# The last four modulations of an encoder trunk, and three smaller orders of its queues

## The chip, the core and the metric

The kernel runs on one core of a Trainium2 chip. Its time is the device time of the program in microseconds (us), the median of the runs. One execution of it was taken by the hardware profiler; all rows below are of that one. Engines are named as the profile names them: PE is TensorE's matmuls and PEld its weight loads, DVE is VectorE, ACT ScalarE, POOL GpSimd, SP the SyncE queue that issues every load and store.

## The reference, cut to what matters

One inference step of a trunk of two layers over 2048 prompt tokens and 32 sample tokens, D_MODEL 1024, float32. Layer 0 is a pooling mixer (windows of 2, 4, 8 and 16 tokens for four groups of 256 channels), layer 1 sliding-window attention with 16 heads and 4 key/value heads. Each branch has a gate path beside it, and each layer is modulated by a vector of the conditioning input c:

```python
def modulation(c, w, b):
    m = jnp.einsum('bd,de->be', jax.nn.silu(c), w) + b
    return jnp.split(m, 3, axis=-1)
...
        for i in range(DEPTH):
            shift, scale, gate = modulation(c, ada_w[i], ada_b[i])
            h = rms_norm(x, norm_g[i]) * (1 + scale[:, None]) + shift[:, None]
            ...
            x = x + gate[:, None] * y
        return rms_norm(x, final_g), ...
```

So a layer needs three modulations of 1024 values for the prompt's c and the same for the sample's: two vectors of 1024 times a matrix of 1024 x 1024, six times in all.

## The kernel before

**Stages.** The prompt is cut into four parts of 512 tokens; part 0 also carries the 32 sample tokens and so has two blocks of 272 columns where the others have one of 512. Activations lie transposed, channels on partitions. The stages are pooling parts 0 to 3, then attention parts 0 to 3. A projection unit is one output tile of 128 channels against all eight input tiles k. Every product of two float32 values is made of three fp32r products (high times high, high times low, low times high; `split_product`, L921), so a unit of 512 columns is 24 matmuls, and it has one PSUM bank of three, `ps_u`, in turn.

**A pooling part** goes through four groups g. A group has the units u0 and u1 (projection tiles `pin`), gate0 and gate1, and two short units z0 and z1 (6 matmuls each) that mix the pooled channels; then come eight output units and the turning of the next part's x. As banks go round by three and z0, z1 follow gate0 and gate1, the next group's u0 takes the bank of gate1. On VectorE a unit's first evacuation (step E1) scales the bank by the norm (L1308); a gate's second (E2) multiplies its silu product into `silu_g` (L1337), and with that the bank is free; PL pools (L1352 to L1377) and PQ subtracts the high part of the pooled tile from it (L1384). Around gate0 VectorE's order is E1 of gate0, PQ, PL, E2 of gate0, PQ, E1 of gate1. After a z unit VectorE multiplies and subtracts again (L1332).

**An attention part** has twenty projection tiles and eight output tiles (`aout`), of which the first four (five in part 0) are kept open in parallel while the last heads finish.

**The hand-made order.** Class `Schedule` writes one list of steps, and every engine walks that list and does its own share of each step, with waits on semaphores that count steps. So where a step stands in the list sets its place in every engine's queue, SP's among them.

**Weights.** A tile is 128x1024. It goes into slot j % RING of four. Tile j is asked for (step WL) right after the last unit that uses tile j - 4. The first time it is loaded raw, split by ScalarE (a copy to the high part, L1525) and GpSimd (the subtraction, L1785) and stored to HBM as two tiles; later it is fetched from there. 24 of the attention tiles are split early, eight in each of pooling parts 1 to 3: step FL loads one raw (L744), FW splits it on ScalarE (L1529) and GpSimd (L1792), FS stores it. There are two buffers for this, so the load of tile i + 2 waits, on SP, for the store of tile i; FL stands right behind the FS before it in the list:

```python
            i = EARLY // 3 * (p - 1) + n
            self.steps.append(("FS", i))
            if i + FORE < EARLY:
                self.steps.append(("FL", i + FORE))
```

**Modulations.** Their weights come in 48 chunks of 512 KB, eight for each modulation. The first 16 chunks are used at the start. The other 32 are spread over the pooling parts, eight steps ADA in each: behind u0 and u1 of groups 0 and 1, behind u1 of group 2 and behind gate0 of groups 0, 1 and 2. A step is four matmuls of 128x32 against 256 columns of the chunk (L952) that sum into a bank of `ps_s`. After a modulation's eight steps ScalarE copies the sums out (step MR, L1538), and in group 3, behind gate0, step MT turns the row of sums into a column with eight matmuls (L964). Three chunk buffers, `load_ada` (L792) issues the next load on SP at each ADA step.

**Waits of a unit.** Before a unit TensorE waits for its tile's weights, and ahead of each k for both halves of that input tile, although these are complete after the first unit of a stage.

## Time and profile before

| what | value |
|---|---|
| median of 3 runs | 1661.25 us (1660.24 to 1665.72) |
| the profiled execution's own time | 1663.97 us |
| its span in the profile | 1662.2 us |
| mean granted TensorE clock | 0.983 |
| HBM | 266.13 MB read, 74.31 MB written, 205 GB/s over the span |

In the page's chain of waits, the chain of work that ended last, TensorE holds 75% of the span, DMA 7%, VectorE 6%, ScalarE 4%. Rows below have these columns: in an order-of-time answer the start in us, the duration in us, engine, line, operation, written tile <- read tiles, shapes, the number of instructions, and in brackets the idle time before it with what ended it. In a table of stretches a number in front of "(x...)" is the busy time in us and the number in brackets is the count of instructions; the last three are the granted clock, the share of DMA engines' time that is busy and the GB/s moved. A product of 128 x 512 is shown with a modelled end; from start to start is the better reading.

### The profile page before, as it was taken

How to read it: one execution, taken by the hardware profiler on the slowest of the kernel's cores; microseconds unless marked ns; L12 is line 12 of the kernel's file. 1: busy time of each engine (PE TensorE's matmuls, PEld its weight loads, DVE VectorE, ACT ScalarE, POOL GpSimd, SP SyncE). 2: the span in 40 equal slices, each digit the busy share in tenths (PEclk: the TensorE clock that was granted, in tenths of full speed). 3: DMA queues.
4: the chain of work that ended last, by engine and by line, in shares of the span. 5: the costliest groups of instructions: out<-in, count | busy, mean ns of one | idle time of the engine just before them, and what ended most of it. 6: DMA issues, size and time to landing. Idle time of an engine off the chain costs nothing.

```text
span 1662.2 us, 28381 instructions
## 1 busy us (share of the span) xinstructions
PE 1572.7 (95%) x9355; PEld 1319.7 (79%) x9355; DVE 826.7 (50%) x2154; ACT 729.9 (44%) x1618; POOL 421.6 (25%) x403
## 2 busy tenths in 40 slices
PE   5899999989999999999889899999899998999997
PEld 2899987777777877888888798888788887888876
DVE  2556335323434344336666634666346664366651
ACT  3444433223232333235555454656436664456642
POOL 0342421112111211112222241333213333123332
PEclk9899999999999999999999999999999999999998
DMA  8787788886888778962222275334463334643313
GB/s 286 267 291 262 265 302 289 299 318 229 281 325 286 272 278 289 335 242 103 103 104 102 102 256 188 142 129 153 151 203 128 128 137 167 211 149 129 131 67 135
DMA packets 174519, 342.10 MB, mean 206 GB/s; under 512 B 22127, under 2 KB 89023, under 8 KB 174126
## 3 DMA queue, kind: packets, MB, share of 16 engines
q1 hardware_dynamic: 174382, 340.29, 58.4%
q8 instruction: 84, 1.38, 0.3%
q14 instruction: 53, 0.43, 0.1%
HBM read 266.13 MB, written 74.31 MB: 205 GB/s over the span
## 4 chain that ended last, share of the span: by engine, by line
PE 75%; DMA 7%; DVE 6%; ACT 4%; issue 3%; SPq 2%; POOL 1%; POOLq 0%; DVEq 0%; ACTq 0%
PE ps_u L921 59%; DMA w_lo_kept<-fore_raw 4%; PE ps_o L1153 4%; PE ps_s L1107 3%; PE ps_t L1126 3%; ACT work L1726 1%; DMA work<-in_x_prompt_dram 1%; DVE work L1453 1%; PE ps_s L921 1%; ACT ps_u L1625 1%; PE ps_s L952 1%; DMA chunks<-in_ada_w_dram 1%; DMA w_raw<-in_pool_w_out_dram 1%; PE ps_t L1166 1%; DVE ps_u L1308 1%
## 5 line engine op out<-in xcount | busy, mean ns | idle before, releaser
L921 PE MATMUL ps_u<-h_all_hi,w_hi 128*128 128x512 f32 (+2 forms) x1440 | 520.4, 361 | 11.9 <-DVE h_all_lo L1238 4.4
L921 PE MATMUL ps_u<-h_all_lo,w_hi 128*128 128x512 f32 (+2 forms) x1440 | 511.2, 355 | 0.0
L921 PE MATMUL ps_u<-h_all_hi,w_lo 128*128 128x512 f32 (+2 forms) x1440 | 510.8, 355 | 0.0
L921 PEld LDWEIGHTS ps_u<-h_all_hi,w_hi 128*128 128x128 f32 x1440 | 274.2, 190 | 66.5 <-issue 22.7
L921 PEld LDWEIGHTS ps_u<-h_all_hi,w_lo 128*128 128x128 f32 x1440 | 274.1, 190 | 36.9
L921 PEld LDWEIGHTS ps_u<-h_all_lo,w_hi 128*128 128x128 f32 x1440 | 274.1, 190 | 34.5
L1308 DVE TENSOR_TENSOR ps_u<-ps_u,rstd_b 128x512 f32<-128x512 f32 (+1 forms) x180 | 107.1, 596 | 274.4 <-PE ps_u L921 266.9
L921 PE MATMUL ps_u<-y_hi,w_hi 128*128 128x512 f32 (+1 forms) x600 | 218.4, 364 | 16.0 <-issue 10.6
L1866 POOL TENSOR_TENSOR work<-work,recip 128x512 f32<-128x512 f32 (+2 forms) x136 | 132.9, 997 | 360.3 <-DVE recip L1470 360.3
L921 PE MATMUL ps_u<-y_hi,w_lo 128*128 128x512 f32 (+1 forms) x600 | 213.2, 355 | 0.0
L921 PE MATMUL ps_u<-y_lo,w_hi 128*128 128x512 f32 (+1 forms) x600 | 212.6, 354 | 0.0
L1726 ACT ACTIVATE work<-work,neg_max 128x256 f32<-128x256 f32 (+1 forms) x272 | 132.1, 487 | 109.1 <-DVE sink_arg L1461 109.1
L1625 ACT ACTIVATE ps_u<-ps_u,wb 128x272 f32<-128x272 f32 (+1 forms) x144 | 73.2, 521 | 160.1 <-DVE ps_u L1308 159.5
L921 PEld LDWEIGHTS ps_u<-y_hi,w_hi 128*128 128x128 f32 x600 | 114.2, 190 | 36.8 <-issue 20.3
L921 PEld LDWEIGHTS ps_u<-y_lo,w_hi 128*128 128x128 f32 x600 | 114.3, 190 | 16.4 <-issue 1.4
L921 PEld LDWEIGHTS ps_u<-y_hi,w_lo 128*128 128x128 f32 x600 | 113.7, 189 | 16.1
L1792 POOL TENSOR_TENSOR fore_raw<-fore_raw,fore_hi 128x1024 fp32r<-128x1024 f32 x24 | 57.5, 2397 | 252.0 <-ACT fore_hi L1529 252.0
L1785 POOL TENSOR_TENSOR w_lo<-w_raw,w_hi 128x1024 fp32r<-128x1024 f32 (+1 forms) x32 | 72.3, 2262 | 145.6 <-ACT w_hi L1525 145.6
L1453 DVE CUSTOM_DVE_ANT_0 work<-ps_s,bias 128x256 f32<-128x256 f32 (+1 forms) x272 | 95.7, 407 | 1.4
L1817 POOL TENSOR_TENSOR acc<-acc,sq 128x512 f32<-128x512 f32 (+1 forms) x48 | 62.7, 1307 | 130.3 <-ACT sq L1667 130.3
L1845 POOL TENSOR_TENSOR y_lo<-acc,y_hi 128x256 fp32r<-128x256 f32 (+1 forms) x72 | 49.2, 684 | 182.2 <-ACT y_hi L1752 182.2
L1625 ACT ACTIVATE work<-ps_u,wb 128x512 f32<-128x512 f32 (+3 forms) x48 | 25.4, 549 | 136.4 <-DVE ps_u L1308 136.4
(210 smaller groups left out, 2237.1 us busy)
## 6 DMA issues: line engine op xcount, KB each, us to landing
w_hi<-w_hi_kept SPq DMA_DIRECT2D x180, 512.0 KB, 4.1
w_lo<-w_lo_kept SPq DMA_DIRECT2D x180, 512.0 KB, 5.2
chunks<-in_ada_w_dram SPq DMA_DIRECT2D x32, 512.0 KB, 6.1
w_hi_kept<-w_hi SPq DMA_DIRECT2D x28, 512.0 KB, 3.3
w_lo_kept<-w_lo SPq DMA_DIRECT2D x28, 512.0 KB, 4.4
w_hi_kept<-fore_hi SPq DMA_DIRECT2D x24, 512.0 KB, 9.1
w_lo_kept<-fore_raw SPq DMA_DIRECT2D x24, 512.0 KB, 10.0
w_raw<-in_pool_w_in_dram SPq DMA_DIRECT2D x16, 512.0 KB, 5.9
```

Source lines behind the costliest of these rows:

```text
L921: last = nc.tensor.matmul(out, w, x, start=(i == 0), stop=(i == n - 1))
L1107: last = nc.tensor.matmul(score_block(it, at + e, k0), q_st[half, q, c0:c0 + P], k[half, d, kc], start=(i == 0), stop=(i == 2))
L1126: last = nc.tensor.transpose(t_flat[:, o:o + P], work[:, a % 2, at * 256 + kt * P:at * 256 + (kt + 1) * P], ident[:, :])
L1153: last = nc.tensor.matmul(ps_o[:, n * 256:n * 256 + 256], v_st[:, d, t + kt, :], pt[:, o:o + 256], start=(i == 0), stop=(i == 2 * len(kts) ...
L1308: V.tensor_tensor(bank[:, 0:w], bank[:, 0:w], rstd_b[:, c0:c0 + w], ALU.mult).then_inc(scaled, 1)
L1453: last = V.tensor_tensor_reduce(out=out, in0=src, in1=b, scale=HEAD_DIM ** -0.5, scalar=LOWEST, op0=ALU.add, op1=ALU.max, accum_out=row_ma ...
L1625: last = A(dst, src, ACT.Identity, bias=wb[:, u["n"], v:v + 1])
L1726: A(x, x, ACT.Exp, bias=neg_max[r, d, at:at + 1], accum_out=row_sum[r, d, at:at + 1])
L1785: G.tensor_tensor(w_lo[:, j % RING, 0:width[j]], w_raw[:, j % RING, 0:width[j]], w_hi[:, j % RING, 0:width[j]].bitcast(F32), ALU.subtract) ...
L1792: G.tensor_tensor(raw.bitcast(F32R), raw, fore_hi[:, i % FORE, :].bitcast(F32), ALU.subtract).then_inc(fore_lo_ready, 1)
L1817: G.tensor_tensor(acc[:, 0:w], acc[:, 0:w], sq[:, 0:w], ALU.add).then_inc(acc_ready, 1)
L1866: last = G.tensor_tensor(x, x, recip[r, d, 2 * n:2 * n + 2].unsqueeze(2).to_broadcast([r.stop - r.start, 2, w]), ALU.mult)
```

## The change

- **Modulations.** Chunks from the 17th on are read as 128 whole rows of `ada_w` (128x1024, contiguous). VectorE takes the ADA step in TensorE's place: for each of the two vectors one operation of 128x1024 multiplies the chunk by a per-partition scalar and adds it to a sum (`mod_sum`) that lies in the x buffer which is free in that part. It signals `ada_added`. Step MT then sums over partitions and turns at once, with sixteen matmuls of 128x128 against a column of ones. Step MR goes for these modulations. New waits: the buffer's earlier content must be stored and squared before the first sum of a modulation, and the next x, and the load of x for attention, wait for `mod_turned`.
- **Early tiles.** FL is no longer behind FS. It stands behind gate0 of the group (for the FS behind u1) or behind the z units (for the FS behind gate1).
- **Tile requests.** The fourth `aout` tile of each attention part goes to a fifth slot that lies in the query buffer `q_st`; it is asked for behind the part's last scores step (S). The other tiles keep the ring of four, counted without it.
- **Unit waits.** TensorE waits for a tile's weights ahead of the tile's first block only, and for the input halves of each k only in the first unit and the first output unit of a stage.

The core of the diff; what is left out passes `slot_of[j]` where `j % RING` stood, waits for `ada_added` where all modulations must be done, and renames a local variable:

```diff
-        load_after = {self.last_unit[j - RING]: j for j in range(RING, len(self.tiles))}
+        self.slot, self.before, held, at = [], [], {}, 0
+        for j, t in enumerate(self.tiles):
+            n = RING
+            if t != ("aout", 3):
+                n, at = at, (at + 1) % RING
+            self.slot.append(n)
+            self.before.append(held.get(n))
+            held[n] = j
+        load_after = {("U", self.last_unit[self.before[j]]): j for j in range(len(self.tiles)) if self.slot[j] < RING and self.before[j] is not None}
+        for j, t in enumerate(self.tiles):
+            if t == ("aout", 3):
+                p = self.units[self.last_unit[j]]["p"]
+                load_after[("S", max(x["a"] for x in self.items if x["p"] == p))] = j
         steps, self.steps = self.steps, []
         for st in steps:
             self.steps.append(st)
-            if st[0] == "U" and st[3] == KT and st[1] in load_after:
-                self.steps.append(("WL", load_after[st[1]]))
+            if (st[0] == "S" or st[0] == "U" and st[3] == KT) and st[:2] in load_after:
+                self.steps.append(("WL", load_after[st[:2]]))
...
             self.steps.append(("ADA", i))
-            if i % KT == KT - 1:
+            if i % KT == KT - 1 and i < self.first:
                 self.steps.append(("MR", i // KT))
 
     def early(self, p, n):
@@ -181,10 +193,13 @@
     def early_out(self, p, n):
 
         if p:
-            i = EARLY // 3 * (p - 1) + n
-            self.steps.append(("FS", i))
-            if i + FORE < EARLY:
-                self.steps.append(("FL", i + FORE))
+            self.steps.append(("FS", EARLY // 3 * (p - 1) + n))
+
+    def early_next(self, p, n):
+
+        i = EARLY // 3 * (p - 1) + n + FORE
+        if p and i < EARLY:
+            self.steps.append(("FL", i))
...
                 if i == 0:
+                    self.early_next(p, 2 * g)
                     self.early(p, 2 * g + 1)
                     s.extend(late + [("PQ", p, g, 1)])
...
             s.extend(late + lower + [("E2", late[0][1])])
+            self.early_next(p, 2 * g + 1)
...
+        q_flat = q_st[:, :, :].rearrange("p a c -> p (a c)")
+        tile_hi = [w_hi[:, i, :] for i in range(RING)] + [q_flat[:, 0:KT * P]]
+        tile_lo = [w_lo[:, i, :] for i in range(RING)] + [q_flat[:, KT * P:2 * KT * P]]
...
+        stage_first = set()
+        for stage in range(2 * PARTS):
+            stage_first.add(next(u["u"] for u in units if u["s"] == stage))
+            stage_first.add(next(u["u"] for u in units if u["s"] == stage and u["kind"] == "out"))
...
+        def mod_sum(m, v):
+
+            return x_of(m - 1)[:, 2 * v:2 * v + 2, 0:PART]
...
+                if slot == RING:
+                    p = units[sched.last_unit[j]]["p"]
+                    sp.wait_ge(s_ready, sum(1 for x in items if x["p"] <= p))
+                else:
+                    tile_used(sp, before_in[j])
...
-                    sp.wait_ge(ada_done, i - CHUNKS + 1)
+                    sp.wait_ge(ada_added, i - CHUNKS - first + 1)
+                if i >= first:
+                    k = i % KT
+                    sp.dma_start(landing[slot], I["ada_w"][l, k * P:(k + 1) * P, what * D_MODEL:(what + 1) * D_MODEL]).then_inc(ada_loaded[slot], 16)
+                    return
...
                     if p < 2:
                         sp.wait_ge(mid_stored[p % 2], 2 * 16 * KT)
                         sp.wait_ge(sq_ready, KT * (p + 3))
+                        sp.wait_ge(mod_turned, len(sched.mods))
...
-                elif kind == "ADA":
+                elif kind == "ADA" and st[1] < first:
 
                     i = st[1]
                     m, half, pair = i // KT, i % KT // 4, i % 4
-                    if m >= 2 and i % KT == 0:
...
+                    if m >= 2:
+                        pe.wait_ge(ada_added, KT * (m + 1) - first)
+                        for k in range(KT):
+                            for v in range(2):
+                                last = nc.tensor.matmul(mod_turn[m][:, 2 * k + v:2 * k + v + 1],
+                                                        mod_sum(m, v)[:, k // 4, k % 4 * P:(k % 4 + 1) * P], ones[:, 0:1], start=True, stop=True)
+                        last.then_inc(mod_turned, 1)
+                        continue
...
-                    if own(j):
+                    if u["b"] == 0 and k_from == 0 and own(j):
                         pe.wait_ge(w_hi_ready, splits(j))
                         pe.wait_ge(w_lo_ready, splits(j))
-                    else:
-                        pe.wait_ge(w_fetched[j % RING], 32 * fetches(j))
+                    elif u["b"] == 0 and k_from == 0:
+                        pe.wait_ge(w_fetched[slot_of[j]], 32 * fetches(j))
...
-                            if u["kind"] != "out":
+                            if u["u"] not in stage_first:
+                                pass
+                            elif u["kind"] != "out":
...
+                elif kind == "ADA" and st[1] >= first:
+
+                    i = st[1]
+                    m, k = divmod(i, KT)
+                    p = m - 2
+                    slot, nth = ada_slot(i)
+                    if k == 0 and p == 0:
+                        dve.wait_ge(ada_done, first)
+                        dve.wait_ge(x_squared, TILES + 1)
+                        dve.wait_ge(x_turned, TILES + 1)
+                    elif k == 0:
+                        dve.wait_ge(mid_stored[(p - 1) % 2], 16 * KT * ((p - 1) // 2 + 1))
+                        dve.wait_ge(sq_ready, KT * p)
+                    if k:
+                        dve.wait_ge(ada_added, i - first)
+                    dve.wait_ge(ada_loaded[slot], 16 * nth)
+                    chunk = landing[slot].rearrange("p (a c) -> p a c", a=2)
+                    for v in range(2):
+                        if k == 0:
+                            last = V.tensor_scalar(mod_sum(m, v), chunk, c_wide[:, k, v:v + 1], None, ALU.mult)
+                        else:
+                            last = V.scalar_tensor_tensor(out=mod_sum(m, v), in0=chunk, scalar=c_wide[:, k, v:v + 1], in1=mod_sum(m, v),
+                                                          op0=ALU.mult, op1=ALU.add)
+                    last.then_inc(ada_added, 1)
...
                         dve.wait_ge(x_turned, xt_at[(p, t)] + 1)
+                        if p:
+                            dve.wait_ge(mod_turned, p + 2)
```

## Rows read from the trace of the kernel before

**Rows 1.** Page, busy us of each engine, share of the span, instructions.

```profile
PE 1572.7 (95%) x9355; PEld 1319.7 (79%) x9355; DVE 826.7 (50%) x2154; ACT 729.9 (44%) x1618; POOL 421.6 (25%) x403
```

**Rows 2.** Stretches of pooling parts 1 to 3: length, busy, clock, DMA.

```profile
227.86:400.62 172.76, 165.70 (x761) 128.74 (x760) 64.92 (x114) 50.72 (x78) 29.70 (x17) 0.97 0.81 287
400.62:569.28 168.66, 162.74 (x755) 126.62 (x754) 67.35 (x114) 50.43 (x78) 29.57 (x17) 0.98 0.82 287
569.28:728.86 159.58, 156.66 (x726) 121.96 (x725) 64.45 (x115) 46.18 (x76) 30.22 (x18) 1.00 0.82 291
```

**Rows 3.** The chain that ended last, in order of time: start, length, link.

```profile
161.45 1.68 PE ps_o L964 x16
...
388.79 5.56 PE ps_u L921 x24
...
395.21 11.13 PE ps_u L921 x48
...
408.59 5.77 PE ps_u L921 x24
...
414.93 5.76 PE ps_u L921 x24
```

**Rows 4.** TensorE in order of time, attention output stages 1 to 3.

```profile
1187.02 0.77 PE L921 MATMUL ps_u<-y_hi,w_hi 128*128 128x512 f32 x1 [3.81 <-issue]
...
1405.97 0.47 PE L921 MATMUL ps_u<-y_hi,w_hi 128*128 128x512 f32 x1 [2.87 <-issue]
...
1622.32 0.47 PE L921 MATMUL ps_u<-y_hi,w_hi 128*128 128x512 f32 x1 [2.89 <-issue]
```

**Rows 5.** Waits of SP's queue by line: us in total, times, longest.

```profile
SPq L744 <- DMA w_lo_kept<-fore_raw: 144.2, 15, 10.7
```

**Rows 6.** TensorE in order of time, norm sums; two records are one matmul.

```profile
407.21 0.36 PE L989 MATMUL ps_o<-ones,sq 128*128 128x1 f32 x2
407.43 0.36 PE L988 MATMUL ps_o<-ones,acc 128*128 128x1 f32 x2
```

**Rows 7.** VectorE, groups by line and shape: busy us, mean ns, idle before.

```profile
L1476 DVE TENSOR_TENSOR pt_lo<-ps_t,pt_hi 128x1024 fp32r<-128x1024 f32 x56 | 68.3, 1220 | 1.9 <-ACT pt_hi L1735 1.4
```

**Rows 8.** VectorE in order of time, part 2, group 0.

```profile
424.97 0.69 DVE L1384 TENSOR_TENSOR q_st<-sq,q_st 128x512 fp32r<-128x512 f32 x1 [0.17 <-ACT q_st L1676]
...
427.05 0.70 DVE L1308 TENSOR_TENSOR ps_u<-ps_u,rstd_b 128x512 f32<-128x512 f32 x1 [1.39 <-PE ps_u L921]
```

**Rows 9.** TensorE in order of time, first matmul of part 2, group 1.

```profile
429.85 0.50 PE L921 MATMUL ps_u<-h_all_hi,w_hi 128*128 128x512 f32 x1
```

**Rows 10.** GpSimd in order of time, parts 0 and 2.

```profile
100.66 1.38 POOL L1785 TENSOR_TENSOR w_lo<-w_raw,w_hi 128x512 fp32r<-128x512 f32 x1 [5.74 <-ACT w_hi L1525]
...
107.64 2.40 POOL L1785 TENSOR_TENSOR w_lo<-w_raw,w_hi 128x1024 fp32r<-128x1024 f32 x1 [5.60 <-ACT w_hi L1525]
...
112.16 2.40 POOL L1785 TENSOR_TENSOR w_lo<-w_raw,w_hi 128x1024 fp32r<-128x1024 f32 x1 [2.12 <-ACT w_hi L1525]
...
425.89 2.40 POOL L1792 TENSOR_TENSOR fore_raw<-fore_raw,fore_hi 128x1024 fp32r<-128x1024 f32 x1 [12.91 <-ACT fore_hi L1529]
```

**Rows 11.** VectorE in order of time, part 0, group 1.

```profile
100.83 1.24 DVE L1352 COPY work<-u_keep 128x16 f32<-128x16 f32 x1
...
109.61 0.45 DVE L1308 TENSOR_TENSOR ps_u<-ps_u,rstd_b 128x272 f32<-128x272 f32 x1 [1.46 <-PE ps_u L921]
...
112.52 2.35 DVE L1332 TENSOR_TENSOR y_lo<-acc,y_hi 128x272 fp32r<-128x272 f32 x1
```

**Rows 12.** Stretch behind the first gap of rows 4, columns as above.

```profile
1187.00:1195.50 8.50, 8.48 (x25) 6.73 (x26) 1.43 (x3) 2.58 (x4) 1.70 (x2) 0.66 0.78 318
```

**Rows 13.** TensorE in order of time, inside a unit of part 2.

```profile
409.56 0.40 PE L921 MATMUL ps_u<-h_all_lo,w_hi 128*128 128x512 f32 x1
409.80 0.39 PE L921 MATMUL ps_u<-h_all_hi,w_lo 128*128 128x512 f32 x1
410.03 0.40 PE L921 MATMUL ps_u<-h_all_hi,w_hi 128*128 128x512 f32 x1
```

More of the change, by code:

```diff
@@ L519, in trunk_kernel @@
         t_flat = ps_t[:, :, :].rearrange("p a b -> p (a b)")
-        mod_bank = [ps_u[0][:, :], ps_u[2][:, :]] + [ps_s[:, m % 2, :] for m in range(2, 6)]
+        mod_bank = [ps_u[0][:, :], ps_u[2][:, :]]
         mod_turn = [ps_u[0] if m == 0 else ps_o for m in range(6)]
@@ L534, in trunk_kernel @@
         w_kept = [sem(f"w_kept{i}") for i in range(RING)]
-        w_fetched = [sem(f"w_fetched{i}") for i in range(RING)]
-        w_hi_ready, w_lo_ready, ada_done = sem("w_hi_ready"), sem("w_lo_ready"), sem("ada_done")
+        w_fetched = [sem(f"w_fetched{i}") for i in range(RING + 1)]
+        w_hi_ready, w_lo_ready, ada_done, ada_added = sem("w_hi_ready"), sem("w_lo_ready"), sem("ada_done"), sem("ada_added")
         prm_turned, prm_ready, c_tanh, c_ready, mod_ready = (
@@ L580, in keeps @@
         def keeps(j):
-            return sum(1 for i in kept if i <= j and i % RING == j % RING and own(i))
+            return sum(1 for i in kept if i <= j and slot_of[i] == slot_of[j] and own(i))
         def fore_done(eng):
@@ L587, in fore_done @@
                 eng.wait_ge(fore_kept[i], 32 * sum(1 for n in range(EARLY) if n % FORE == i))
-            eng.wait_ge(ada_done, KT * len(sched.mods))
+            eng.wait_ge(ada_added, KT * len(sched.mods) - first)
         def fetches(j):
-            return sum(1 for i in range(j + 1) if i % RING == j % RING and not own(i))
+            return sum(1 for i in range(j + 1) if slot_of[i] == slot_of[j] and not own(i))
         def tile_used(eng, j):
@@ L753, in load_tile @@
                 t = tiles[j]
-                if j >= RING:
-                    tile_used(sp, j - RING)
-                    if own(j - RING):
-                        sp.wait_ge(w_kept[j % RING], 32 * keeps(j - RING))
-                load_raw(t, w_raw[:, j % RING, :], raw_loaded[j % RING])
+                if before_in[j] is not None:
+                    tile_used(sp, before_in[j])
+                    if own(before_in[j]):
+                        sp.wait_ge(w_kept[slot_of[j]], 32 * keeps(before_in[j]))
+                load_raw(t, w_raw[:, slot_of[j], :], raw_loaded[slot_of[j]])
             def keep_tile(j):
@@ L1060, in _ @@
                             last = split_product(bank[:, 0:w], [
-                                (w_hi[:, slot, k * P:(k + 1) * P], w_lo[:, slot, k * P:(k + 1) * P],
+                                (hi[:, k * P:(k + 1) * P], lo[:, k * P:(k + 1) * P],
                                  xh[:, k, c0:c0 + w], xl[:, k, c0:c0 + w])], k == 0, k == KT - 1)
@@ L1080, in _ @@
                     pe.wait_ge(k_prev, n)
-                    first = 0 if p else 1
-                    for b in range(TILES + 1 - first):
-                        last = nc.tensor.transpose(s_flat[:, b * P:(b + 1) * P], kv_t[:, (first + b) * P:(first + b + 1) * P], ident[:, :])
+                    b0 = 0 if p else 1
+                    for b in range(TILES + 1 - b0):
+                        last = nc.tensor.transpose(s_flat[:, b * P:(b + 1) * P], kv_t[:, (b0 + b) * P:(b0 + b + 1) * P], ident[:, :])
                     if p == 0:
```

43 lines of the change are left out of this document (22 added, 21 removed).

## The prediction

> **What bounds the kernel now.** I read the page's busy shares first: TensorE is busy 95% of the span, VectorE 50% [rows 1]. So a microsecond counts only if it lies on TensorE's line or in one of its gaps. Next the table by stage, cut at the first matmul of each stage, which shows the three pooling parts that carry eight modulation steps each (parts 1 to 3): 172.76, 168.66 and 159.58 us for the same products [rows 2]. Then the chain of waits: a projection unit is 24 matmuls, two in a row take 11.13 us, so 5.57 a unit, and units with a modulation step between them start 6.34 apart [rows 3]. A step costs TensorE 0.77 us. Last, the gaps: in the output stage of the last three attention parts TensorE stands for 3.81, 2.87 and 2.89 us before the fifth output tile [rows 4], and SP spent 144.2 us behind the stores of early-split tiles [rows 5].
>
> The profiled run took 1663.97 us round a span of 1662.2; the median of the runs shown is 1661.25, 2.7 lower. I sum against 1663.97 and take 2.7 off. A measurement of this kernel can tell about 0.3% (5 us) from no change.
>
> **The steps leave TensorE.** 32 steps of 0.77 are 24.6 us, 6.2 in each pooling part (the first part's blocks are narrower, the step the same four matmuls; I take the same price). The four evacuations of row sums on ScalarE go too; nothing waits for them now, so they count nothing.
>
> **The turning gets longer.** Eight turning matmuls, sixteen records, take 1.68 us [rows 3]. Now there are sixteen of 128x128 against one column. The norm's sums are of that very form, and one is issued every 0.22 us [rows 6]: 16 make 3.5. That is 1.8 us more, four times, on TensorE, with nothing beside it: +7.2.
>
> **VectorE gets 64 operations of 128x1024.** The nearest row is the 1024-column split, 1.22 us [rows 7]; one operand there is in PSUM, so this bounds the price from below where a port is contended. A step is 2.4 us, 77 us in all. VectorE's average allows it; what counts is the place. In VectorE's order the third step of a group stands behind the second low-part subtraction (L1384) and ahead of the first evacuation of the second gate unit (L1308). The next group's first projection reuses that gate's bank, so it waits for the gate to be finished. In part 2 the last subtraction starts at 424.97, the second gate's evacuation at 427.05 [rows 8], the next projection at 429.85 [rows 9]: 2.80 us from evacuation to projection. VectorE's slack before it is 1.39 us [rows 8], and without TensorE's step the gate would even end 0.77 earlier.
>
> With 2.4 us of new work from 425.60 (0.63 behind the start of L1384, as operations follow each other in that list) the evacuation would start at 428.0 and the projection at 430.8, 0.95 late. But GpSimd's split of an early tile starts at 425.89 and takes 2.40 [rows 10], between the two halves. What that means is in part 0: GpSimd's split from 112.16 takes 2.40 [rows 10], and a subtraction of two SBUF operands on VectorE, started at 112.52, takes 2.35 for 272 columns [rows 11], ending with it. Both new operands of a step lie in SBUF too. Who goes first when both queue: GpSimd's split at 100.66 [rows 10] stands against a VectorE stream without a gap, and the copy of 16 columns at 100.83 takes 1.24 [rows 11]. So GpSimd gets in between two VectorE instructions. The step is then 1.22, 2.40, 1.22: done at 430.4, projection at 433.2, **3.35 late**. The Trainium skill (SBUF — State Buffer, Who interferes with whom) speaks against this change here: a VectorE instruction with two SBUF inputs contends with a GpSimd one that reads SBUF, and issue order decides who blocks. The rows above agree with it; who goes first when both queue it does not say, and by it alone the sum lies anywhere between my two ends, 1645 and 1680.
>
> So for parts 1 to 3 both ends are +0.95 and +3.35 a group. I take 3.35, since the two rows with both engines waiting look like that. Per part: three groups, 10.05, less five other steps, 3.85, plus 1.8 for turning: +8.0, over three parts **+24.0**. (At the low end: 2.85 - 3.85 + 1.8 = +0.8 each, +2.4.)
>
> Part 0 is tighter, as each unit has two blocks. Between a group's first gate and its last silu product VectorE shows 1.46 us idle that a delay can use up, before 109.61 [rows 11]. Two steps fall into this stretch, 2.4 and, with a split between the halves (at 107.64 one begins where the step would [rows 10]), 4.8: 7.2 - 1.46 = 5.7 us late, in three groups; two more steps saved outside give 1.5 back, turning takes 1.8: **+17.4** (low end, no split between: 3.3 a group, +10.2).
>
> **Clock.** In parts 1 to 3 TensorE then stands 4.2 us nine times (from 429.0 to 433.2). After the 3.81 us gap [rows 4] the granted clock was 0.66 over the next unit, which took 8.4 instead of 5.7 us [rows 12], in part at the 1.2 GHz level; after the gap of 2.87 nothing of the kind is seen. So 0 to 2.7 us each; I take 0.7, **+6**. The longer turning may cost as much once or twice; it stays in the range.
>
> **SP's requests move.** The raw load of the next early tile was issued right behind the store of the one before it in its slot, and held SP, with weight requests and modulation loads queued behind it, until that store had landed [rows 5]. It moves about one unit later (behind the first gate, or the last product pair of a group), past the weight request of that unit and ahead of a modulation load. The store is then nearly done. Parts 1 and 2 are longer than part 3 by 13.2 and 9.1 us [rows 2]; turning the next x explains four times 0.85 of each (units 388.79 and 395.21 apart by 6.42 against 5.57 [rows 3]). The other 9.8 and 5.7 are late tiles, late x and the slow clock behind them. DMA is busy 0.82 there [rows 2], so I give back 14 and 2 more in part 3, whose steps waited on their chunks: **-16** (bounds -8 and -18). The chunk now comes by 4 KB rows and is wanted some 5 us later on VectorE.
>
> **The extra slot.** The fourth output tile goes to the query buffer, asked for once the part's last scores are done; the fifth takes a ring slot free since the last gate. That removes 3.81 + 2.87 + 2.89 = 9.6 [rows 4] and the slow clock behind the first, 2.7 [rows 12], and perhaps some of the third: **-13** (bounds -9.6 and -14). Next there is the bank of the first output tile, evacuated well inside the three short products that follow.
>
> **Unit waits.** TensorE drops up to 16 waits in most units. Within one k, where no wait stands, the third product starts 0.24 us behind the second; the first of the next k, which has the waits, starts 0.23 behind that [rows 13], and 48 in a row take 11.13 [rows 3], 0.232 each over 16 such borders. A wait that is already met shows no price on either side: 0.
>
> New waits on VectorE (stored x, squares, chunk loaded) stand in front of the step, and the evacuations of the next units queue behind them; the store and the chunk are issued a unit or more ahead, so 0, at most the 7 us of one late chunk. x's load for attention waits for all turnings, long done.
>
> Sum: 1663.97 + 24.0 + 17.4 + 6 - 16 - 13 = 1682.4; less 2.7, **1680** for the runs.
>
> **Rivals.** (1) GpSimd does not get in: VectorE's two halves run back to back. For it: they are issued together, and each starts before GpSimd is ready. Against it: the copy at 100.83. Then +2.4 + 10.2 - 16 - 13 = -16.4 and no gap over 2 us, so no clock: 1645, **faster**. It decides at the nine third steps: at 2.4 us the loss per group is 0.95, at 4.8 it is 3.35; nine groups, three of part 0 and the clock grow with it, so the total crosses zero about 16.4 / (12 + 6/2.4) = 1.1 above 2.4, at 3.5 us a step. (2) VectorE's work hides altogether: -24.6 + 7.2 - 29 = -46, 1615. Against it is the 1.39 us of slack for 2.4 of work. (3) SP is held by another wait (the early store, whose split now ends later), and of its 16 us only the 8 of the low bound come back: with the lock 1688. (4) Losses and returns cancel: GpSimd gets in, but only in the six groups of two parts (-7.2), the clock doesn't fall (-6), and part 0 loses half of what lies between its ends (-3.6): 1663.
>
> **Chances.** Forecast 1680 (own range 1667 to 1694, by the bounds) with (3): 0.54. Rival 1: 0.30, a range of 1636 to 1652. Rival 2: 0.06. Rival 4: 0.10, within 5 us of no change. So slower 0.54, same 0.10, faster 0.36. Range 1640 to 1694: it leaves out rival 2, the lowest part of rival 1 and a little above.
>
> **What would show it.** In the new profile the third step of a group should be two operations of 1.2 and 3.6 us with GpSimd's split between, and TensorE should wait 4 us for L1337's product at the end of three groups in each of parts 1 to 3; part 3 should be longer than 159.58, parts 1 and 2 about as long as before. Turning should take 3.5 us, the gap before the fifth output tile should be gone. If those operations are 1.2 and 1.2, rival 1 holds. If part 0 grows by under 10 us, its sum was wrong.

## The result, and the profile after

The changed kernel takes 1699.6 us, the median of 4 runs (1696.0 to 1703.4), against 1663.4 for the kernel before on the same chip: 1.0219 of its time (95% interval 1.0186 to 1.0253), 36 us slower. The forecast was 1680 and 1694 at the upper end of the range; the direction was right and the size was not. The profiled execution took 1703.4 us round a span of 1701.6, which is the longest of the four runs, so its rows show some 4 us more than the median.

The page's busy times of the changed kernel (rows 1 are those of before):

```profile
PE 1585.6 (93%) x9163; PEld 1351.1 (79%) x9163; DVE 923.5 (54%) x2218; ACT 727.2 (43%) x1614; POOL 431.6 (25%) x403
```

VectorE has 97 us more, where 64 operations were added. TensorE has 192 records less (128 matmuls gone and 32 added, two records each) and still 13 us more of busy time. Busy time that grows while work shrinks points at the clock.

The table of stretches of the changed kernel, cut at the first matmul of each stage: pooling part 0, then parts 1 to 3, which answer to [rows 2]. Columns are length, busy time by engine, granted TensorE clock, DMA share and GB/s.

```profile
51.69:256.97 205.28, 183.69 (x1320) 180.59 (x1321) 116.58 (x254) 74.26 (x144) 68.44 (x35) 0.92 0.70 241
256.97:436.00 179.03, 167.30 (x713) 134.96 (x711) 89.15 (x130) 50.08 (x77) 32.76 (x17) 0.92 0.79 277
436.00:610.87 174.87, 163.20 (x708) 132.20 (x707) 91.55 (x130) 49.94 (x77) 32.78 (x17) 0.95 0.80 277
610.87:782.22 171.35, 159.74 (x679) 128.56 (x678) 88.68 (x131) 45.70 (x75) 33.40 (x18) 0.95 0.78 271
```

Part 0 was 178.0 us before (from 49.86 to 227.86) and is 27.3 longer. Parts 1 to 3 are 6.3, 6.2 and 11.8 longer, 24.3 together. The four attention parts are 14.2 shorter (926.7 to 912.5 from the first matmul of the first to TensorE's last). The first projection starts 1.8 later. That is the whole difference of the spans: 27.3 + 24.3 - 14.2 + 1.8 = 39.2 of 39.4. The granted clock of the pooling parts fell from 0.97, 0.98 and 1.00 [rows 2] to 0.92, 0.95 and 0.95.

VectorE in order of time in part 2, group 0, the place that [rows 8] show before (start, duration, instruction, idle time in front):

```profile
458.06 0.68 DVE L1409 SCALAR_TENSOR_TENSOR silu_g<-silu_g,ps_u 128x512 f32<-128x512 f32 x1
458.92 0.69 DVE L1456 TENSOR_TENSOR q_st<-sq,q_st 128x512 fp32r<-128x512 f32 x1 [0.17 <-ACT q_st L1750]
459.53 4.62 DVE L1283 SCALAR_TENSOR_TENSOR x_odd<-chunks,c_wide,x_odd 128x1024 f32<-128x1024 f32 x2
464.07 0.69 DVE L1380 TENSOR_TENSOR ps_u<-ps_u,rstd_b 128x512 f32<-128x512 f32 x1
466.11 0.69 DVE L1409 SCALAR_TENSOR_TENSOR silu_g<-silu_g,ps_u 128x512 f32<-128x512 f32 x1 [1.36 <-ACT silu_g L1715]
```

GpSimd in order of time at the same place, and TensorE's first matmul of the next group:

```profile
459.84 3.22 POOL L1866 TENSOR_TENSOR fore_raw<-fore_raw,fore_hi 128x1024 fp32r<-128x1024 f32 x1 [11.48 <-ACT fore_hi L1601]
```

```profile
466.86 0.79 PE L959 MATMUL ps_u<-h_all_hi,w_hi 128*128 128x512 f32 x1 [3.88 <-DVE silu_g L1409]
```

This is the picture that was forecast. The step's two operations take 4.62 us with GpSimd's split in them (the split itself shows 3.22 instead of 2.40 [rows 10]; it starts behind the step's first operation and waits for it). The second gate is evacuated from 464.07, its silu product follows 2.04 later, and TensorE has stood for 3.88 us. The same stall of 3.8 to 3.9 is there in all nine groups of parts 1 to 3.

What the forecast had nearly left out comes behind the stall. Stretches of 8.6 and 7.3 us that hold the first unit behind two such stalls, in parts 1 and 2, columns as above:

```profile
289.80:298.40 8.60, 8.54 (x25) 6.75 (x26) 2.68 (x5) 1.26 (x2) 0.00 (x0) 0.64 0.71 266
466.80:474.10 7.30, 7.24 (x25) 5.84 (x26) 2.67 (x5) 1.26 (x2) 0.00 (x0) 0.77 0.99 380
```

The unit's 24 matmuls take 7.3 to 8.7 us instead of 5.8, at a mean granted clock between the two levels of 1.2 and 2.4 GHz. Over the nine units it is 17.0 us (2.8, 2.2, 1.6, 1.5, 1.5, 1.5, 2.7, 1.6 and 1.6 longer than the same units before).

Two more things changed as planned. Turning is longer; this is the one of part 3, where 3.67 us for 32 records stood as 3.5 in the forecast. In parts 0 to 2 it is 4.52, 4.14 and 4.89, as the clock falls in the middle of it; the stretch is the second half of the one in part 2, where TensorE is busy throughout at a granted clock of 0.50:

```profile
722.71 3.67 PE L1001 MATMUL ps_o<-ones,x_even 128*128 128x1 f32 x32
```

```profile
549.00:551.30 2.30, 2.30 (x12) 2.30 (x13) 2.10 (x4) 1.03 (x2) 0.00 (x0) 0.50 1.00 371
```

And the gap before the fifth output tile [rows 4] is gone. TensorE in order of time in attention part 1: the last product of the fourth tile, read from the query buffer, and the first of the fifth.

```profile
1235.31 0.40 PE L959 MATMUL ps_s<-y_hi,q_st 128*128 128x512 f32 x1
1235.55 0.40 PE L959 MATMUL ps_u<-y_hi,w_hi 128*128 128x512 f32 x1
```

### The profile page after: what moved, and what is told of

The parts are those of the page before. It is cut to its first block, busy times and chain, and to the rows that moved or that the text cites. A ratio compares the mean times of both kernels' runs of the same rounds, so it can differ in the third digit from the quotient of the medians.

```text
span 1701.6 us, 26049 instructions
## 1 busy us (share of the span) xinstructions
PE 1585.6 (93%) x9163; PEld 1351.1 (79%) x9163; DVE 923.5 (54%) x2218; ACT 727.2 (43%) x1614; POOL 431.6 (25%) x403
## 4 chain that ended last, share of the span: by engine, by line
PE 75%; DVE 12%; ACT 6%; issue 3%; DMA 2%; POOL 1%; SPq 1%; DVEq 0%; ACTq 0%; POOLq 0%
PE ps_u L959 59%; PE ps_o L1199 4%; PE ps_s L1153 3%; PE ps_t L1172 3%; DVE x_odd L1283 2%; DVE x_even L1283 2%; ACT ps_u L1699 1%; PE ps_s L959 1%; ACT work L1800 1%; DVE work L1430 1%; DVE work L1525 1%; DVE ps_u L1380 1%; PE ps_o L1001 1%; PE ps_t L1212 1%; ACT silu_g L1715 1%
## 5 line engine op out<-in xcount | busy, mean ns | idle before, releaser
L959 PE MATMUL ps_u<-h_all_hi,w_hi 128*128 128x512 f32 (+2 forms) x1440 | 531.1, 369 | 48.3 <-DVE silu_g L1409 44.1
L959 PE MATMUL ps_u<-h_all_lo,w_hi 128*128 128x512 f32 (+2 forms) x1440 | 521.9, 362 | 0.0
L959 PE MATMUL ps_u<-h_all_hi,w_lo 128*128 128x512 f32 (+2 forms) x1440 | 521.1, 362 | 0.0
L959 PEld LDWEIGHTS ps_u<-h_all_hi,w_hi 128*128 128x128 f32 x1440 | 282.8, 196 | 91.0 <-DVE silu_g L1409 48.7
L959 PEld LDWEIGHTS ps_u<-h_all_hi,w_lo 128*128 128x128 f32 x1440 | 282.8, 196 | 39.1
L959 PEld LDWEIGHTS ps_u<-h_all_lo,w_hi 128*128 128x128 f32 x1440 | 283.4, 197 | 37.1
L959 PE MATMUL ps_u<-y_hi,w_hi 128*128 128x512 f32 (+1 forms) x584 | 211.9, 363 | 5.5 <-POOL y_lo L1919 5.3
L959 PE MATMUL ps_u<-y_hi,w_lo 128*128 128x512 f32 (+1 forms) x584 | 207.4, 355 | 0.0
L959 PE MATMUL ps_u<-y_lo,w_hi 128*128 128x512 f32 (+1 forms) x584 | 207.1, 355 | 0.0
L1866 POOL TENSOR_TENSOR fore_raw<-fore_raw,fore_hi 128x1024 fp32r<-128x1024 f32 x24 | 66.4, 2766 | 266.7 <-ACT fore_hi L1601 253.1
L959 PEld LDWEIGHTS ps_u<-y_hi,w_lo 128*128 128x128 f32 x584 | 110.4, 189 | 15.7
```

The costliest lines, as they stand in the source:

```text
L959: last = nc.tensor.matmul(out, w, x, start=(i == 0), stop=(i == n - 1))
L1866: G.tensor_tensor(raw.bitcast(F32R), raw, fore_hi[:, i % FORE, :].bitcast(F32), ALU.subtract).then_inc(fore_lo_ready, 1)
```

## The experiments

Two theories stood against each other. **Place**: all that is lost comes from where the VectorE steps stand, as a stall with the slow clock behind it, and the other edits give back time. **Load or other edits**: VectorE has no room for 77 us more wherever they stand, or the moved requests cost something too. Each run below gives its median beside the kernel before on the same chip (1665.6, 1665.1, 1666.7 and 1665.0 in the four sets of runs). The other columns are stage lengths of the profiled execution alone, from first matmul to first matmul, attention up to TensorE's last:

| kernel | median, us | part 0 | parts 1 to 3 | attention |
|---|---|---|---|---|
| before | 1663.4 | 178.0 | 501.0 | 926.7 |
| changed | 1699.6 | 205.3 | 525.3 | 912.5 |
| modulations back on TensorE | 1631.1 | 178.3 | 478.8 | 911.6 |
| before, modulations on VectorE only | 1713.4 | 205.0 | 520.9 | 924.1 |
| changed, third step moved | 1638.9 | 191.7 | 473.5 | 912.2 |
| changed, no split within the third step | 1668.5 | 204.8 | 481.1 | 912.8 |
| changed, two steps moved | 1642.0 | 190.3 | 475.9 | 912.8 |
| before, extra slot only | 1649.9 | 179.0 | 503.4 | 910.7 |
| before, later early loads only | 1643.4 | 178.5 | 478.7 | 925.6 |
| before, unit waits dropped only | 1665.1 | 181.5 | 499.7 | 926.1 |
| changed, early loads back | 1697.4 | 202.6 | 520.8 | 910.9 |
| changed, third step moved, early loads back | 1666.9 | 190.3 | 505.1 | 912.1 |
| changed, matmuls in the stall | 1684.2 | 203.2 | 502.0 | 912.5 |
| TensorE in part 0, VectorE behind z | 1629.1 | 180.7 | 477.1 | 911.9 |
| the same, turning in three | 1623.4 | 181.1 | 471.0 | 911.5 |

### Modulations back on TensorE, the rest kept

```diff
-            if i % KT == KT - 1 and i < self.first:
+            if i % KT == KT - 1:
                 self.steps.append(("MR", i // KT))
...
-                elif kind == "ADA" and st[1] < first:
+                elif kind == "ADA":
...
-                elif kind == "ADA" and st[1] >= first:
...
```

> The changed kernel with its last four modulations on TensorE again as before (steps, evacuation and turning); tile requests, extra slot, later early loads and unit waits stay. Theory 'place' (the VectorE steps cost all that is lost): pooling part 0 is back at 178.0 us, parts 1 to 3 give back 11 against the kernel before (34.4 of stalls + 13.3 of slow clock + 6.2 of turning - 18.2 of steps saved = 35.7 against 24.3 measured), attention gives back 14.2: 1663.4 - 11 - 14 = 1638. Rival 'other edits' (the later requests or the slot cost time too, so the steps cost less than that): above 1655.

Measured: 1631.05 us, 0.9806 of before (0.9786 to 0.9826). Part 0 is back at 178.3. So the other three edits are worth 35 us and the VectorE steps cost 69 on top of them. "Other edits" falls; "place" had the total 7 too high, as parts 1 to 3 give back 22, not 11.

### Only the modulations, on the kernel before

```diff
-                elif kind == "ADA":
+                elif kind == "ADA" and st[1] < first:
...
+                elif kind == "ADA" and st[1] >= first:
```

> The kernel before with nothing but its last four modulations on VectorE. Theory 'place': + 27.3 in part 0 and + 35.7 in parts 1 to 3 = 1726, attention as before. Rival 'other edits': the steps alone cost less, under 1705. If early loads behind the stores hold SP less now that the steps come later, it may lie some 5 below the first figure.

Measured: 1713.4 us, 1.0297 (1.0276 to 1.0319). Part 0 is 27.0 longer, parts 1 to 3 are 19.9 longer, not 35.7. The steps alone cost 48 on the kernel before and 69 on the kernel with the other edits: 48 - 35 would make the changed kernel 1678, and it is 1699.6. Something that the other edits give back is swallowed when the steps are on VectorE.

### The third step of a group behind the second z unit

```diff
-                    if g < 3:
-                        self.ada(1)
-                    else:
+                    if g == 3:
                         s.append(("MT", 2 + p))
...
             self.early_next(p, 2 * g + 1)
+            if g < 3:
+                self.ada(1)
```

> The changed kernel, but the third step of a group stands behind the second z unit instead of behind the first gate; the same 64 operations on VectorE. Theory 'place': TensorE's stall of 3.82 us and the slow unit behind it (1.5 on average) go nine times in parts 1 to 3, 48 us; in part 0 some 5.3 of a group's 8.5 go, three times, and the 3.16 that the second step costs before the second gate's second block stays: 1699.6 - 48 - 16 = 1636. Rival 'load' (VectorE has no room for 77 us more, the delay turns up at the next evacuation): 1690 to 1700.

Measured: 1638.9 us, 0.9848 (0.9833 to 0.9863): the same 64 operations, 12 of the 32 steps moved three units down the list, and 61 us less than the changed kernel. VectorE in order of time behind the z units in part 1 (the last subtraction of the group, the step, the next group's first evacuation):

```profile
275.84 0.69 DVE L1404 TENSOR_TENSOR y_lo<-sq,y_hi 128x512 fp32r<-128x512 f32 x1
276.45 2.48 DVE L1283 SCALAR_TENSOR_TENSOR x_even<-chunks,c_wide,x_even 128x1024 f32<-128x1024 f32 x2
279.74 0.70 DVE L1380 TENSOR_TENSOR ps_u<-ps_u,rstd_b 128x512 f32<-128x512 f32 x1 [0.81 <-PE ps_u L959]
```

Behind the step VectorE waits 0.81 us for TensorE, where TensorE waited 3.88 for it. "Load" falls for parts 1 to 3. In part 0 13.7 us stay.

### GpSimd's split kept out of the third step

```diff
                     pool.wait_ge(fore_hi_ready, i + 1)
+                    if i % 8 in (1, 3, 5):
+                        pool.wait_ge(ada_added, 8 * (i // 8 + 1) + (3, 6, 8)[i % 8 // 2])
```

> The changed kernel, but in parts 1 to 3 GpSimd's second split of a group waits for the third step, so that it doesn't fall between that step's two operations. Theory 'place with the port': the step takes 2.45 us instead of 4.6, TensorE stands 1.7 to 1.8 instead of 3.8 nine times, -19, and the slow units behind the stalls go with it in part or whole, -6 to -13: 1668 to 1675; part 0 as in the changed kernel. Rival 'place alone' (GpSimd's split does not lengthen the step, the two operations take 4.6 anyway): 1699, stalls of 3.8.

Measured: 1668.5 us, 1.0003 (0.9981 to 1.0024), 31 less than the changed kernel. Ten runs lie between 1658.2 and 1670.4 and the profiled one is the shortest, so its table of stages flatters it by 10. VectorE, TensorE and the stretch behind, in part 2, group 0:

```profile
439.79 2.47 DVE L1283 SCALAR_TENSOR_TENSOR x_odd<-chunks,c_wide,x_odd 128x1024 f32<-128x1024 f32 x2
442.18 0.69 DVE L1380 TENSOR_TENSOR ps_u<-ps_u,rstd_b 128x512 f32<-128x512 f32 x1
```

```profile
444.97 0.49 PE L959 MATMUL ps_u<-h_all_hi,w_hi 128*128 128x512 f32 x1 [1.72 <-DVE silu_g L1409]
```

```profile
444.90:450.70 5.80, 5.73 (x25) 4.69 (x26) 2.68 (x5) 1.26 (x2) 0.00 (x0) 1.00 1.03 410
```

The same two operations take 2.47 us without the split between them, the stall is 1.72 instead of 3.88, and the unit behind runs at a granted clock of 1.00. "Place alone" falls: GpSimd's split made the step 2.15 us longer, nine times 19. In this execution all nine slow units behind the stalls went too. That they go in every execution is not shown: over the ten runs the mean granted clock lies between 0.970 and 0.979, and in the profiled one it is 0.979.

### Two steps behind the z units

```diff
-                if g < 2:
-                    self.ada(1)
-                elif g == 2 and i:
+                if g < 2 and i == 0:
                     self.ada(1)
...
-                    if g < 3:
-                        self.ada(1)
-                    else:
+                    if g == 3:
...
+            if g < 3:
+                self.ada(2)
```

> The changed kernel, with the step behind the second projection unit and the step behind the first gate both moved behind the second z unit of the group. Theory 'place': parts 1 to 3 as with one step moved (27 under the kernel before), and in part 0 the 3.2 to 3.7 us that the second step cost in each of three groups go, with the slow unit of 1.6 behind each: part 0 then differs from before by - 5.3 for the steps and + 4.9 for the turning, 178. 1639 - 14 = 1625. Rival 'load': two steps in a row, 4.9 us, hold up the next group's evacuations as much: 1639 or more.

Measured: 1642.0 us, 0.9853 (0.9816 to 0.9891). A miss by 17: the rival was right in part 0. There VectorE and TensorE show, in group 1:

```profile
89.35 7.14 DVE L1281 SCALAR_TENSOR_TENSOR x_odd<-chunks,c_wide,x_odd 128x1024 f32<-128x1024 f32 x4
96.40 0.15 DVE L1376 COPY wb<-ps_u 128x2 f32<-128x2 f32 x1
96.47 0.78 DVE L1378 TENSOR_TENSOR ps_u<-ps_u,rstd_b 128x272 f32<-128x272 f32 x2
```

```profile
97.49 0.39 PE L957 MATMUL ps_u<-h_all_hi,w_hi 128*128 128x272 f32 x1 [2.45 <-ACT work L1697]
```

Two steps in a row take 7.14 us, not 4.9, since GpSimd's split of a ring tile, 2.60 us from 90.29, falls among them, and the stall only moves to the second projection unit. Neither of the two places tried is cheap in part 0.

### The extra slot, the later loads and the unit waits, each alone on the kernel before

The three edits are those of the diff above, each by itself (tile slots and requests; `early_next`; the conditions in front of TensorE's waits).

> The kernel before with only the extra slot for the fourth output tile. The forecast's term: attention parts 1 to 3 lose their gaps of 3.81, 2.87 and 2.89 and the slow unit behind the first, -13: 1652. By the changed kernel's own stages, where 15 went: 1650. Rival 'the next tile is late instead': 1660 or more.

> The kernel before with only the early tiles' raw loads moved later in the list. The forecast's term -16, all in pooling parts 1 to 3: 1649. By the run with the modulations put back on TensorE, where these parts are 22 shorter: 1643. Rival 'SP waits for something else in its place': 1660 or more.

> The kernel before with only the unit waits dropped. The forecast's price is 0: 1665, every unit of 24 matmuls at 5.73 us as before. Rival 'a wait costs issue time': units shorter than 5.70 and 1655 or less.

Measured: 1649.9 us for the slot, 0.9905 (0.9873 to 0.9937), so 15 less; 1643.4 for the later loads, 0.9862 (0.9831 to 0.9894), 22 less, all of it in parts 1 to 3; 1665.1 for the waits, 0.9996 (0.9978 to 1.0014), nothing. The first is 2 and the second 6 above the forecast's terms of 13 and 16, the third is the forecast's 0.

### The early loads back behind the stores, in the changed kernel

```diff
+            self.steps.append(("FS", i))
+            if i + FORE < EARLY:
+                self.steps.append(("FL", i + FORE))
...
-            self.early_next(p, 2 * g + 1)
```

> The changed kernel, with the early tiles' raw loads back right behind the stores, as before. Theory 'covered' (where TensorE stands for VectorE in each group, the late tiles arrive meanwhile, so the move is worth nothing there): the run with the modulations alone, 1713.4, less the slot's 15.2: 1698, no change to the changed kernel. Rival, the forecast's term: 16 more, 1716; by the run of the move alone 22 more, 1721.

Measured: 1697.4 us, 1.0203 (1.018 to 1.0225), the changed kernel's own time. SP's wait for these stores, in the changed kernel and then with the loads back (us in total, times, longest):

```profile
SPq L773 <- DMA w_lo_kept<-fore_raw: 59.2, 15, 7.4
```

```profile
SPq L768 <- DMA w_lo_kept<-fore_raw: 134.5, 15, 11.5
```

The move takes 75 us of waiting behind stores from SP, which then waits longer for TensorE to free a tile's slot (764 us with the loads back, 865 in the changed kernel). But the same move that is worth 22 us alone is worth nothing in this kernel. Either TensorE's stalls for VectorE cover what SP makes late, or the chunks that come late no longer stop TensorE once VectorE uses them. The next run takes the stalls away and keeps the loads behind the stores.

### The third step moved, and the early loads back

The edit is shown against the kernel with the third step moved.

```diff
+            self.steps.append(("FS", i))
+            if i + FORE < EARLY:
+                self.steps.append(("FL", i + FORE))
...
-            self.early_next(p, 2 * g + 1)
             if g < 3:
                 self.ada(1)
```

> The kernel with the third step behind the second z unit, with the early tiles' raw loads back right behind the stores. Theory 'covered' (the later loads are worth nothing in the changed kernel because TensorE stands there for VectorE anyway): here there is no such stall, so the move is worth what it is alone, 22 us: 1660. Rival 'off the line' (what SP's waiting made late were the chunks, and these no longer stop TensorE once VectorE uses them): no change, 1639 to 1643.

Measured: 1666.9 us, 1.0009 (0.9988 to 1.0031), 28 above the same kernel with the later loads. VectorE, TensorE and SP's issues in part 1, group 1:

```profile
291.70 2.48 DVE L1278 SCALAR_TENSOR_TENSOR x_even<-chunks,c_wide,x_even 128x1024 f32<-128x1024 f32 x2 [6.41 <-DMA chunks<-in_ada_w_dram]
```

```profile
290.48 0.47 PE L954 MATMUL ps_u<-h_all_hi,w_hi 128*128 128x512 f32 x1 [0.37 <-DMA w_lo<-w_lo_kept]
301.62 1.19 PE L954 MATMUL ps_u<-q_st,w_hi 128*128 128x512 f32 x2 [5.35 <-DVE q_st L1451]
```

```profile
272.82 0.66 SPq L873 DMA_DIRECT2D w_lo_kept<-fore_raw  x1
283.17 0.38 SPq L768 DMA_DIRECT2D fore_raw<-in_attn_w_in_dram  x1
284.69 0.43 SPq L819 DMA_DIRECT2D chunks<-in_ada_w_dram  x1
```

Without the stalls, SP issues nothing from 273.48 to 283.17, between the store and the load behind it, and asks for the next chunks after that. VectorE waits 6.41 us for a chunk, and TensorE 5.35 us for VectorE behind that; a weight tile is late too. "Off the line" falls. In the changed kernel with its loads back no engine waits for a chunk in parts 1 to 3, as these transfers land while TensorE stands for VectorE in any case: the gain was covered by the loss, and that is what lies between 1678 and 1699.6.

### Matmuls in the stall

```diff
+                    if u["kind"] == "u" and u["i"] == 0 and u["g"] and 1 <= p:
+                        claim("s")
+                        for n in range(16):
+                            nc.tensor.matmul(ps_s[:, 0, 0:PART], h_all_hi[:, n % KT, 0:P], h_all_hi[:, n % KT, 0:PART], start=True, stop=True)
```

> The changed kernel, with 16 more matmuls of 128x512 on TensorE (3.7 us, their result is used by nothing) in front of the first projection unit of groups 1 to 3 in pooling parts 1 to 3, where it stands for 3.8 us. Theory 'the standing lowers the clock': the stall ends as late as before, but the nine units behind it take 5.73 at a granted clock of 1.0 instead of 6.6 to 8.7, 13.3 us in sum: 1686. Rival 'the slow units have another cause': 1699 or, where the extra matmuls come in the way, more.

Measured: 1684.2 us, 1.0113 (1.0091 to 1.0135), 15 less than the changed kernel, with 144 matmuls more. TensorE in order of time in part 1, group 1, and the stretch of the unit behind:

```profile
285.35 3.87 PE L1052 MATMUL ps_s<-h_all_hi 128*128 128x512 f32 x16
289.40 0.50 PE L959 MATMUL ps_u<-h_all_hi,w_hi 128*128 128x512 f32 x1 [0.17 <-DVE silu_g L1413]
```

```profile
289.35:295.10 5.75, 5.70 (x25) 4.67 (x26) 2.67 (x4) 1.27 (x2) 0.00 (x0) 1.00 1.00 381
```

The unit still waits for the silu product and starts as late as in the changed kernel; only the granted clock is 1.00, where the changed kernel's stretch from 289.80 had 0.64, and it takes 5.8 us instead of 8.7. All nine units are like this one, 17.0 us shorter together. The slow units are the price of standing.

### Part 0's modulation on TensorE, and the turning in three

The first edit puts part 0's modulation on TensorE again, as in the kernel before, and keeps VectorE for parts 1 to 3 with the third step behind the z units. The second also cuts the turning in three.

```diff
+        self.te = 3 * KT
...
-                elif kind == "ADA" and st[1] >= first:
+                elif kind == "ADA" and st[1] >= te:
...
+            if g < 3 and p:
+                self.ada(1)
```

> The changed kernel with the modulation of part 0 on TensorE again (and its turning), and in parts 1 to 3 on VectorE with the third step of a group behind the second z unit. By stages: the run with all modulations on TensorE, 1631, and in parts 1 to 3 the 5.3 us by which the run with the third step moved is shorter there: 1626. Rival 'no gain of VectorE over TensorE, for the longer turning and its slow unit eat it': 1630 to 1634.

```diff
+            if g == 3 and p:
+                s.append(("MQ", 2 + p, 0))
...
+                    for k in ((0, 1, 2), (3, 4, 5), (6, 7))[q]:
+                        for v in range(2):
+                            last = nc.tensor.matmul(mod_turn[m][:, 2 * k + v:2 * k + v + 1],
```

> As the kernel of the run before in this list, but in parts 1 to 3 the sixteen turning matmuls are cut in three (6, 6 and 4), behind the second projection and each of the two gate units of group 3. Theory 'one-column matmuls in a row lower the clock': the slow unit behind the turning (7.3 to 8.4 us in place of 5.7) goes three times, 4.5 to 6: 1621. Rival 'their number counts, not the row': 1626.

Measured: 1629.1 us, 0.9782 (0.9761 to 0.9802), and 1623.4 us, 0.9745 (0.9724 to 0.9766). The first is 3 above its expectation and can't be told from the run with all modulations on TensorE, 1631.1. The second is 6 below the first, and 43 below the kernel before on the same chip. It lies halfway between what its theory and its rival gave, so the time alone does not choose. The stretch that holds the end of the turning and the unit behind in part 1 (the first kernel), and the one between the second and the third piece (the second):

```profile
333.00:341.00 8.00, 8.00 (x34) 6.54 (x34) 2.47 (x6) 1.58 (x2) 2.37 (x1) 0.79 0.61 222
```

```profile
333.50:339.50 6.00, 6.00 (x31) 4.96 (x30) 3.81 (x9) 2.62 (x4) 1.79 (x1) 1.00 0.99 384
```

The three pieces of the second kernel, TensorE in order of time:

```profile
325.44 1.39 PE L1016 MATMUL ps_o<-ones,x_even 128*128 128x1 f32 x12
332.34 1.39 PE L1016 MATMUL ps_o<-ones,x_even 128*128 128x1 f32 x12
339.23 0.95 PE L1016 MATMUL ps_o<-ones,x_even 128*128 128x1 f32 x8
```

They are 3.73 us together, no less than the 3.63 in one piece in part 1; what goes is the slow unit behind, in all three parts. But one piece does not always bring it. Here are a turning in one piece, in part 1 of the run in which GpSimd's split is kept out of the third step, and the stretch that holds its end and the unit behind:

```profile
355.07 3.63 PE L1001 MATMUL ps_o<-ones,x_even 128*128 128x1 f32 x32
```

```profile
357.80:365.80 8.00, 8.00 (x40) 6.68 (x40) 3.16 (x7) 2.19 (x3) 2.40 (x1) 1.00 0.63 204
```

In the nine profiled kernels that turn in one piece, the unit behind is slow in 20 of the 27 cases in parts 1 to 3. What sets the other seven apart is not shown.

## Why the prediction was wrong

**The step that failed is the clock term.** The forecast gave +6, 0.7 for each of nine stalls, and nothing for part 0. The units behind the nine stalls are 17.0 us longer; the three behind the longer turning in parts 1 to 3 are 2.6, 1.9 and 1.5 above the 5.4 us that a unit at full clock shows there from its first product to its last, 6.0 together; and in part 0 the units and half-units behind stalls and turning are 10.5 longer. So the term measures 33.5. It had its row: after the gap of 3.81 [rows 4] the unit took 2.7 more [rows 12]. The forecast had stalls of 4.2 and took a quarter of that price, because nothing followed the gap of 2.87; nine of nine stalls of 3.8 to 3.9 were followed by a slow unit of 1.5 to 2.8. Its clock term weighed only two of the three gaps. The stretches of the kernel before behind the gaps of 2.87 and 2.89:

```profile
1405.90:1411.80 5.90, 5.83 (x25) 4.79 (x26) 1.42 (x2) 3.38 (x6) 2.58 (x2) 1.00 1.01 401
1622.30:1629.70 7.40, 7.38 (x25) 5.94 (x26) 0.00 (x0) 2.08 (x3) 2.57 (x2) 0.77 0.97 386
```

Behind the third, hardly longer than the second, the unit took some 1.5 more. Both runs on the term agree: with matmuls in the stall 15 us go, with a stall of 1.72 the slow units go in the profiled execution. The Trainium skill (TensorE: Matmul & The Clock Gate, Why this matters for your kernels) warns of idle gaps between bursts of matmuls, and these rows agree with it.

**VectorE's late gate was right.** Forecast: the step takes 4.8 us with GpSimd's split inside and the projection comes 3.35 late; measured 4.62 and a stall of 3.88, of which the saved 0.76 is to be taken off, 3.1. The two-sided bound was the right one to keep: without the split the step is 2.47, as the low end had it. The Trainium skill's rule on two SBUF inputs and a reading GpSimd (SBUF — State Buffer, Who interferes with whom) agrees with 4.62 against 2.47. The order that it leaves open is the same in all nine groups here: the split that queues behind the first operation goes before the second.

**Steps and turning were right.** A step's going gave 0.64 to 0.77 against 0.77 forecast. Against the kernel before with only the later loads, whose parts 1 to 3 have no late tiles, nine stalls of 3.82 net of the old spacing are 34.4, less 18.2 for 24 steps, plus 7.2 for turning (5.4 forecast): 23.4 in parts 1 to 3 against +24.0.

**Part 0 was right but for the clock.** +17.4 forecast, +27.3 measured, of which 10.5 are longer units behind stalls and turning. Another 1.1 is the part's first unit, which stands in front of every modulation step on VectorE. That leaves 15.7.

**SP's term was too small and had the wrong cause.** By the terms above, parts 1 to 3 should be 23.4 + 17.0 + 6.0 = 46.4 longer and are 24.3, so 22 came back, where the forecast had 16. That is the whole of what the later loads take off alone. But with the loads put back as before the time is the same (1697.4), and with the modulations alone parts 1 to 3 got back no less. What came back is time that late chunks, tiles and x had cost and that now lies under VectorE's stalls, with or without the move. The row of such a late tile in the kernel before is a gap of 2.13 behind the turning of part 2, with a slow unit after it; the later loads alone remove both:

```profile
506.22 2.13 issue
508.35 8.16 PE ps_u L921 x24
```

The forecast put a loss and a gain into one sum although both sit in front of the same unit, where only the later of two waits counts. This error made the forecast 6 too high, not too low.

**The extra slot and the unit waits were right:** 14.2 in the trace and 15 in the run alone against 13; nothing against 0.

Rival 1 is out, as GpSimd did get in. The third step's move comes within 24 us of rival 2 with the same operations (1638.9 against 1615, most of the rest being part 0). Rival 3 is out, as the move alone gave 22, and rival 4, as all nine groups had the split and the slow unit. The sum of terms as measured is 23.4 + 17.0 + 6.0 - 22 - 14.2 + 15.7 + 10.5 + 1.1 + 1.8 = 39.3, the spans' 39.4. The 1.8 before the first projection is not explained by any edit there; that start lay between 49.9 and 54.0 us in the profiled executions of kernels whose steps up to it are the same.

## What to carry to other kernels

Price a stall of the engine that sets the end by what follows it too: here 3.9 us of standing cost 5.4 to 6.7. Ask for each added operation which engine it can block or be blocked by at that moment, as GpSimd's split did here, and move it to the place in the list where its engine waits for the bound engine anyway; the same 64 operations cost 61 us less with 12 steps three units later. And don't add a loss and a gain that end in front of the same instruction: one covers the other.

## What the runs showed of the hardware

- Sixteen one-column matmuls in a row can lower TensorE's granted clock though the engine has no idle time: 0.50 over the second half of one such row, 0.79 over 8 us that hold the end of another and the unit behind. It was so in 20 of 27 cases (1.00 in the stretch of one of the other seven), and in none of three where the same 16 stand in three groups between units.
- GpSimd's recorded duration can hold a wait: the split took 3.22 where it became ready during VectorE's first operation, 2.40 in the kernel before [rows 10].
- A wait that is already met costs TensorE nothing that can be measured: 16 fewer in most units left 0.9996 (0.9978 to 1.0014).
